# Output projection of a decoder block as seven products of quarters instead of one product

## The reference

```
(shift, scale, gate) = c @ W_mod + b_mod
u = x * (1 + scale) + shift
[q|k|v|z_a|B|C|xc|z_b|g_a|g_b] = u @ W_in
y_a = differential attention of q, k, v, 8 heads, RMS norm, * silu(z_a)
y_b = B * causal_conv3(C * xc) * silu(z_b)
h   = sigmoid(g_a) * (y_a @ P_a) + sigmoid(g_b) * (y_b @ P_b)
out = h @ W_out                                    # 512 x 2048 times 2048 x 2048
r   = 2**0.25 * x + gate * out
y   = (r - mean(r)) * rsqrt(var(r) + 1e-5) * ln_gain + ln_bias
```

## Time and profile before

| | us |
|---|---|
| median of 3 runs | 1496.1 (1493.0 to 1501.31) |
| the profiled execution, device time | 1492.94 |
| its span, first to last instruction | 1491.0 |
| matmuls in the output stage O0 | 768 |
| PE busy in the span | 1469.9 |

### The profile page before, as it was taken

One profiled execution on the slowest core, in us unless ns is written; L12 is line 12 of the kernel. 1 busy time (PEld: TensorE's weight loads), 2 busy tenths in 40 slices (PEclk: granted clock), 3 DMA queues, 4 the chain that ended last, 5 costly groups with the idle time before them and its releaser, 6 DMA issues.

```text
span 1491.0 us, 18556 instructions
## 1 busy us (share of the span) xinstructions
PE 1469.9 (99%) x6648; PEld 1212.9 (81%) x6648; DVE 887.9 (60%) x1234; ACT 525.0 (35%) x764; POOL 54.3 (4%) x101
## 2 busy tenths in 40 slices
PE   7999999999999999999999999999999999999996
PEld 6788888888888888888888888888887888788885
DVE  6988852286584865848658486585335233534447
ACT  2334532343543435434354343542231212421120
POOL 0000000000001000010000100000000000000000
PEclk9999999999999999999999999999999999999998
DMA  9999542352535525355253552524522322463222
GB/s 356 392 344 324 178 128 85 92 163 78 162 91 169 162 79 160 91 169 161 81 159 91 169 161 80 160 92 148 197 85 85 113 84 90 161 258 112 84 85 113
DMA packets 213164, 223.47 MB, mean 150 GB/s; under 512 B 8577, under 2 KB 160513, under 8 KB 212353
## 3 DMA queue, kind: packets, MB, share of 16 engines
q1 hardware_dynamic: 200736, 176.72, 36.1%
q0 software_dynamic: 11280, 39.85, 8.5%
q10 hardware_dynamic: 1106, 6.32, 1.0%
HBM read 213.43 MB, written 9.44 MB: 149 GB/s over the span
## 4 chain that ended last, share of the span: by engine, by line
PE 96%; DVE 2%; DMA 1%; issue 0%; ACT 0%; SPq 0%; DVEq 0%; ACTq 0%; POOLq 0%
PE acc L1468 30%; PE acc L1469 30%; PE acc L1470 30%; PE sc L1613 1%; PE sc L1468 1%; DMA raw<-in_w_in 1%; PE sc L1470 1%; PE sc L1469 1%; PE sc L1622 1%; PE misc L1470 1%; PE misc L1468 1%; PE misc L1469 1%; PE sc L1533 0%; DMA sig_b<-g_late 0%; DVE w_lo L908 0%
## 5 line engine op out<-in xcount | busy, mean ns | idle before, releaser
L1468 PE MATMUL acc<-act_hi,w_hi 128*128 128x512 f32 x1344 | 528.3, 393 | 2.2 <-DVE act_lo L983 2.2
L1470 PE MATMUL acc<-act_hi,w_lo 128*128 128x512 f32 x1344 | 524.1, 390 | 0.0
L1469 PE MATMUL acc<-act_lo,w_hi 128*128 128x512 f32 x1344 | 523.9, 390 | 0.0
L586 ACT ACTIVATE w_hi<-raw 128x1024 fp32r<-128x1024 f32 (+2 forms) x258 | 267.9, 1045 | 704.7 <-PE acc L1470 560.4
L908 DVE TENSOR_TENSOR w_lo<-raw,w_hi 128x1024 fp32r<-128x1024 f32 x254 | 306.3, 1214 | 330.5 <-ACT w_hi L586 328.6
L1468 PEld LDWEIGHTS acc<-act_hi,w_hi 128*128 128x128 f32 x1344 | 252.8, 188 | 57.7 <-DVE act_lo L983 3.0
L1470 PEld LDWEIGHTS acc<-act_hi,w_lo 128*128 128x128 f32 x1344 | 252.7, 188 | 53.3
L1469 PEld LDWEIGHTS acc<-act_lo,w_hi 128*128 128x128 f32 x1344 | 252.9, 188 | 51.8 <-issue 0.2
L1468 PE MATMUL acc<-w_hi,act_hi 128*128 128x512 f32 x368 | 143.3, 389 | 0.0
L1470 PE MATMUL acc<-w_hi,act_lo 128*128 128x512 f32 x368 | 143.2, 389 | 0.0
L1469 PE MATMUL acc<-w_lo,act_hi 128*128 128x512 f32 x368 | 143.2, 389 | 0.0
(11 more groups left out here) (212 smaller groups left out, 1150.0 us busy)
## 6 DMA issues: line engine op xcount, KB each, us to landing
raw<-in_w_in SPq DMA_DIRECT2D x258, 256.0 KB, 6.7
raw<-in_w_tail SPq DMA_DIRECT2D x32, 1024.0 KB
raw<-in_w_in SPq DMA_DIRECT2D x25, 1024.0 KB
w_mod_in<-in_w_mod SPq DMA_DIRECT2D x32, 512.0 KB, 8.8
w_mod_in<-in_w_mod SPq DMA_DIRECT2D x16, 1024.0 KB, 7.6
gate_in<-in_w_mod POOLq DMA_DIRECT2D x32, 512.0 KB, 4.1
bias_w<-in_w_in POOLq DMA_DIRECT2D x48, 256.0 KB, 3.3
res<-in_x ACTq DMA_DIRECT2D x1, 4096.0 KB, 13.6
```

Of the source, the lines that this page charges most:

```text
L586: return act.activation(dst, src, ACT.Copy)
L1468: pe.matmul(dst, a_hi, b_hi, start=first, stop=False)
L1469: pe.matmul(dst, a_hi, b_lo, start=False, stop=False)
L1470: return pe.matmul(dst, a_lo, b_hi, start=False, stop=last)
```

## The change

The output projection is cut into quarters: the 2048 rows of W_out into two halves (B1x, B2x), its columns into two (Bx1, Bx2), and `h` into two halves of tokens and two of rows (A11, A12, A21, A22), each quarter of `h` 256 tokens by 1024. Seven products replace eight. With S1 = A21+A22, S2 = S1-A11, S4 = A12-S2, S3 = A11-A21 and T1 = B12-B11, T2 = B22-T1, T3 = B22-B12, T4 = T2-B21 (signs are turned in places), their order is A11 B11, A12 B21, S1 T1, S2 T2, S4 B22, S3 T3, A22 T4; below they are called M0 to M6.

- A product has eight steps. A step is 128 rows by 1024 columns of weights (again 1024 elements for each partition) and 12 matmuls: four banks (2 token tiles by 2 column blocks) by 3. M6 goes bank by bank instead of step by step.
- Two sets of four banks are used: `acc`, and `sc` with `misc`. M3, M5 and M6 go on in the banks of M0, and M4 in those of M2. ACT copies a partial result out (`keep`, M0, M2 and M3), and DVE adds or subtracts a finished one (`join`, after M1, M4 and M5). M2 waits for the join after M1, and M6 for the join after M5.
- Plain quarters of weights (M0, M1, M4) come in pieces of 0.5 MB through a ring of four places in `raw`. B12 (4 MB) goes into `chain`. The sums are made there: ACT turns the sign, and POOL issues DMAs of 0.5 MB that add to what is in SBUF (`accum_op`), eight for M2, eight for M3, eight for M5 (into the ring) and eight for M6, at most four in flight. Six more add `x` to a gated quarter of `res`, two add `ln_bias`.
- The sums of `h` are made by DVE (`sums_of_h`).
- `gate` is divided by ALPHA, so that `x` is added as it is, and the norm's epsilon by ALPHA squared. For the first two token tiles ACT does the normalization (`Identity` with scale and bias, 2048 elements), DVE multiplies by `ln_g`, and a DMA adds `ln_bias`.
- `h_hi` and `h_lo` of whole tiles go; `hi_part` and `lo_part` (two each for a product, 1024 elements) come.

The ACT program (cut):

```diff
+            def turn_t2(i):
+                r = piece_of(S3_T3, i)
+                before = RING[(r - SLOTS) // HK]
+                act.wait_ge(lo_ready, step_of(before, (r - SLOTS) % HK) + 1 + RAW_START)
+                act.activation(ring(r), chain[:, i], ACT.Copy, scale=-1.0).then_inc(t3_begun, 1)
+                act.wait_ge(lo_ready, step_of(S2_T2, i) + 1 + RAW_START)
+                act.wait_ge(t3_begun, i + 1)
+                act.activation(chain[:, i], chain[:, i], ACT.Copy, scale=-1.0).then_inc(t2_turned, 1)
...
-                    round_at(S0, 0, 0, 4 * e + s + LEAD)
+                    if 4 * e + s + LEAD < 4 * SHORT:
+                        round_at(S0, 0, 0, 4 * e + s + LEAD)
+                    else:
+                        out_hi(A11_B11, 4 * e + s + LEAD - 4 * SHORT)
                     if s == 0:
                         act.wait_ge(late_back[e], 16)
                         for n in range(4):
                             act.activation(sig_b[:, n, :], sig_b[:, n, :], ACT.Sigmoid).then_inc(sig_ready, 1)
-                    if e == 0:
-                        act.wait_ge(half_done, S0 + BASE)
-                        h_hi(2 * s)
-                        h_hi(2 * s + 1)
-                    else:
-                        h_hi(8 + s)
+                    elif e == 0 and s < 3:
+                        hi_part(A11_B11, s - 1)
+                    if e == 1:
+                        turn_b12(s)
...
+            for i in range(5):
+                out_hi(S4_B22, i)
+            keep(S2_T2, "C12")
+            out_hi(S4_B22, 5)
+            hi_part(S3_T3, 0)
+            turn_t2(0)
+            out_hi(S4_B22, 6)
+            hi_part(S3_T3, 1)
+            turn_t2(1)
+            out_hi(S4_B22, 7)
+            turn_t2(2)
+            turn_t2(3)
+            for i in range(4):
+                out_hi(S3_T3, i)
+                turn_t2(4 + i)
```

The DVE program from M5 on:

```diff
+            for i in range(4):
+                out_lo(S3_T3, i)
+            join(S4_B22, "C12")
+            times_gate("C12", 1)
+            out_lo(S3_T3, 4)
+            lo_part(A22_T4, 0)
+            out_lo(S3_T3, 5)
+            lo_part(A22_T4, 1)
+            for i in (6, 7):
+                out_lo(S3_T3, i)
+            for i in range(4):
+                out_lo(A22_T4, i)
+            stats_of("C12")
+            settle()
+            for t in range(2):
+                spread(t)
+            for i in (4, 5, 6):
+                out_lo(A22_T4, i)
+            join(S3_T3, "C22")
+            out_lo(A22_T4, 7)
+            times_gate("C22", 2)
...
+            last_quarter(0)
+            for t in range(2):
+                dve.wait_ge(z_made, t + 1)
+                for c0 in (0, MID):
+                    dve.tensor_tensor(res[:, t, c0:c0 + MID], res[:, t, c0:c0 + MID], ln_g[:, c0:c0 + MID], ALU.mult
+                                      ).then_inc(scaled, 1)
+            stats_of("C22")
+            dve.wait_ge(ln_b_in, 16)
+            for t in (2, 3):
+                for j in ((1,) if t == 2 else (2, 3)):
+                    last_quarter(j)
+                settle()
+                spread(t)
```

POOL's queue, and PE's waits:

```diff
+            def add_weights(m, i, row, col):
+                e = added(m, i)
+                if e >= 4:
+                    pool.wait_ge(added_in[e % 4], 16 * (e // 4))
+                k = row * HK + i
+                dst = ring(piece_of(m, i)) if m == S3_T3 else chain[:, i]
+                pool.dma_start(dst, w_tail[k * P:(k + 1) * P, col * MID:(col + 1) * MID].rearrange(
+                    "p (a c) -> p a c", a=2), accum_op=ALU.add).then_inc(added_in[e % 4], 16)
...
+            for i in range(HK):
+                pool.wait_ge(t3_begun, i + 1)
+                add_weights(S3_T3, i, 0, 0)
+                pool.wait_ge(t2_turned, i + 1)
+                add_weights(A22_T4, i, 1, 0)
+            add_x("C12", 1)
+            add_x("C22", 2)
...
+            def wait_bank(m, j):
+                if m == A11_B11:
+                    pe.wait_ge(bank_drained[j], S_BLOCK0 + SHORT + BASE)
+                elif m == S1_T1:
+                    pe.wait_ge(m_added, j + 1)
+                elif m in (S2_T2, S4_B22, S3_T3):
+                    pe.wait_ge(m_copied, 4 * (m - S2_T2) + j + 1)
+                elif m == A22_T4:
+                    pe.wait_ge(m_added, 8 + j + 1)
```

More of the change, by code:

```diff
@@ new lines, in keep, with turn_b12 @@
+            def keep(m, name):
+                for j in range(4):
+                    if j < 3:
+                        act.wait_ge(m_full, 3 * m + j + 1)
+                    else:
+                        act.wait_ge(half_done, step_of(m + 1, 0) + BASE)
+                    copy(quarter_of(name, j // 2, j % 2), bank(m, j)).then_inc(m_copied, 1)
+            def turn_b12(n):
+                act.wait_ge(chain_in[n], 16)
+                both = chain[:, 2 * n:2 * n + 2, :, :]
+                act.activation(both, both, ACT.Copy, scale=-1.0).then_inc(b12_turned, 1)
@@ L868, in _ @@
[L868 to L879, removed]
@@ new lines, in _ @@
+            keep(S2_T2, "C12")
[11 more added lines that the diff above has]
+                turn_t2(4 + i)
+            out_hi(S3_T3, 4)
+            hi_part(A22_T4, 0)
+            out_hi(S3_T3, 5)
+            hi_part(A22_T4, 1)
@@ L886, in _ @@
+            for t in range(2, NT):
+                root(t)
         @block.vector
@@ L1365, in _, with out_lo @@
             close(4 + HEADS)
[L1368 to L1371, removed]
+            def out_lo(m, i):
+                f = step_of(m, i)
+                dve.wait_ge(hi_ready, f + 1)
+                end = m == A22_T4 and i < HK // 2
+                dve.tensor_tensor(w_end_lo[:, i] if end else w_lo[:, f % SLOTS], weights(m, i),
+                                  (w_end_hi[:, i] if end else w_hi[:, f % SLOTS]).bitcast(F32), ALU.subtract
+                                  ).then_inc(lo_ready, 1)
@@ new lines, in wait_full, with join @@
+            def wait_full(m, j):
+                if j < 3:
+                    dve.wait_ge(m_full, 3 * m + j + 1)
+                else:
+                    dve.wait_ge(half_done, step_of(m + 1, 0) + BASE)
+            def join(m, name):
+                for j in range(4):
+                    dst = quarter_of(name, j // 2, j % 2)
+                    wait_full(m, j)
+                    dve.wait_ge(m_copied, {"C11": 0, "C22": 4, "C12": 8}[name] + j + 1)
+                    if name == "C12":
+                        ins = dve.tensor_tensor(dst, dst, bank(m, j), ALU.subtract)
+                    else:
+                        ins = dve.tensor_tensor(dst, bank(m, j), dst, ALU.add if name == "C11" else ALU.subtract)
+                    ins.then_inc(m_added, 1)
@@ new lines, in _ @@
+            lo_part(S1_T1, 0)
+            out_lo(A12_B21, 5)
+            lo_part(S1_T1, 1)
+            out_lo(A12_B21, 6)
+            for b in range(2):
+                sums_of_h(S2_T2, b)
+            out_lo(A12_B21, 7)
+            for i in range(3):
+                out_lo(S1_T1, i)
+            join(A12_B21, "C11")
+            for i in (3, 4):
+                out_lo(S1_T1, i)
+            lo_part(S2_T2, 0)
+            out_lo(S1_T1, 5)
+            lo_part(S2_T2, 1)
+            out_lo(S1_T1, 6)
```

413 lines of the change are left out of this document (309 added, 104 removed).

## The result

| | before | after |
|---|---|---|
| time, median of 8 runs | 1493.49 us (1492.67 to 1501.31) | 1507.13 us (1505.40 to 1508.19) |
| ratio of times, 95% interval | | 1.0081 [1.0065, 1.0098] |
| span of the profiled execution | 1491.0 us | 1506.3 us |
| matmuls | 6648 | 6552 |

The kernel became 0.8% slower: 96 matmuls fewer, and 13.6 us more between the medians (12.1 us by the ratio). Forecast was 1494.5 us, no change. What came is the first rival, slower by the price of the adding transfers, which had a chance of 0.30 and 1504 to 1507 us. That 1507.13 lies at the edge of these bounds is partly luck: they were counted from a median before of 1496.1 us, where eight runs gave 1493.49, and as a change of span the rival said 8 to 11 us, where 15.3 came.

What follows compares the result with a forecast made beforehand. PE was taken as the bound: span 1491.0 - 21.8 (matmuls) + 0.6 (M0) + 0.6 (M2) + 7.9 (M5) + 6.5 (M6) + 2.8 (tail) + 1.5 (adds) = 1489.3; from the 1496.1 median, 1494.5 us, range 1484 to 1511.

Steps and rivals of the forecast that it cites:

- the first rival: Adding transfers on POOL's queue from M4's sixth step are the bound; at 2.47 us each 1504 to 1507 us; chance 0.30.
- M1 term: M1 waits some 1.5 us because eight adds, its plain pieces and `ln_g` share the DMA engines.
- The transfers that add: Step bounding a 0.5 MB add between 1.24 us (plain) and 2.47 us (twice the bytes); added 1.5 us at M1.
- I take 2.1: Price chosen for each 0.5 MB add, 2.1 us, because the second read doubles but the write doesn't.
- the prediction's own inequality: Between M4's sixth step and M6, 18 adds are in time only up to 2.1 us each.
- the third rival: Second `sig_b` comes 2 us later, M0 starts 2 to 3 us later, 1497 us; chance 0.45 together with the forecast.
- M5, ACT's order: In M5 hi, lo and two turns run in series, 4.42 us a step where PE needs 2.72: +7.9 us.
- M6, DVE's order: Before M6, DVE has 23.8 us without a gap from M5's lo 3 to the join: PE waits +6.5 us.
- The clock: PE's clock may fall after 6.5 us standing before M6; up to 2.8 us that costs nothing, DVE being behind.
- The tail: After M6, DVE's last quarter starts 2.8 us after PE's end, then 11.4 us as before: +2.8 us.
- The second rival: PE stays the bound, stalls of M5 and M6 half or less and DVE's tail lateness gone: 1484 us; chance 0.25.
- The sum with no price for adding: Span of 1487.7 us from matmuls saved and the waits at M0, M2, M5, M6 and tail, without M1's 1.5.

Runs made afterwards that it cites:

- plain_all: The changed kernel with every adding transfer made a plain one of the same bytes, sums left out: 1494.32 us, ratio 0.9990 to the kernel before.
- loads_later: The changed kernel with SP's loads of `ln_g` and of `x` for C21 moved behind four pieces of M4: 1503.43 us, ratio 1.0055 to the kernel before.
- entry: The changed kernel with ACT's turns of B12 behind the first three hi, DVE's first sum of `h` behind the draining: 1505.93 us, ratio 1.0066.
- orders: `loads_later` plus reordered ACT hi and turns, M5's and M6's adds, DVE joins and C12 statistics, M6's weights in order: 1497.15 us, ratio 1.0006.
- parked2: `entry` plus four -T2 pieces made in M3 in empty buffers, adds begun earlier, turns and adds reordered, 2 MB loads later: 1486.05 us, ratio 0.9940.

## Why the prediction was wrong, by its own steps

Where each product began, by the prediction's sum with its M1 term of 1.5 us, and in the trace:

| mark | predicted | measured | behind |
|---|---|---|---|
| M0 starts | 1305.9 | 1307.7 | 1.8 |
| M1 starts | 1329.2 | 1333.2 | 4.0 |
| M2 starts | 1351.6 | 1357.3 | 5.7 |
| M5 starts | 1417.0 | 1422.6 | 5.6 |
| M6 starts | 1453.0 | 1467.1 | 14.1 |
| PE ends | 1474.8 | 1491.9 | 17.1 |
| end | 1489.3 | 1506.3 | 17.0 |

**The step that failed is "The transfers that add", and in it "I take 2.1".** An add cost 2.49 us, the upper of the two bounds worked out from the rows (2.47). The reason given for 2.1, that only the read is doubled and the write isn't, did not make it cheaper: the engines were full at half the rate of plain pieces. By the prediction's own inequality, from 2.1 us on M5's last hi and C12's sums come late, and they did, M5's hi by far the more: the two later waits in M5 and the longer stand before M6 are what `plain_all` takes away. The middle value was moreover the one at which nothing is late, a choice that should have made me look twice; with the upper end the sum was 1499 to 1502 of span. A second term was too low, what the clock costs; it is priced below. The rule that stood beside it is told of the adding step of a ReduceScatter, which has two source reads on one ring and so half the rate of a copy, measured there at 1.93 times (the Trainium skill, "Collectives: The Full Stack", The bandwidth ceiling). The runs agree with its factor: 2.49 for 1.24 us is 2.0. That the two reads are the cause, no run here shows.

**M1's wait** was the same mis-sized price: 1.5 us taken, 3.5 measured (4.3 at 2.47 us by the prediction). Its sum was also taken at its low end: 8 x 2.1 and ten pieces at 1.24 to 1.45 us are 29.2 to 31.3 us in a stretch of 28, so 1.2 to 3.3. `loads_later` and `plain_all` each take the wait away. Between M1 and M2 the wait came as worked out, 0.4 us for 0.6, but M1's matmuls took 1.7 us more than 21.8, which the sum didn't have: the clock was down after the wait.

**M0** came 1.8 us late: `sig_b`'s second round starts on ACT at 1294.11, not 1292.2. Half of the 1.9 us is that POOL issued its load at 1287.16 and not 1286.2, since `h` was added up at 1286.8 and not 1285.8; the other half is that ACT had it 6.95 us after the issue, not 6.0, which is the third rival (2 to 3 us), right in kind. In `entry` `sig_b` comes as late (1294.17) and PE doesn't wait: the orders of ACT and DVE remove the wait. What that is worth, some 2 us by the ratios, is not clear of the noise.

**M5, ACT's order** was right: round 4.45 for 4.42 us, waits of PE 1.5, 1.6, 1.6 and 2.9 us for 1.35, 1.70, 1.70 and 3.1. What came on top is two waits for adds (3.4 us; all of these counted from start to start, less 0.23) and matmuls further apart (3.9 us).

**M6, DVE's order.** The prediction had DVE work 23.8 us without a gap from its fourth lo of M5 to the join. It took 31.8, with four gaps:

```profile
1434.50 1.22 DVE L1631 TENSOR_TENSOR w_lo<-raw,w_hi 128x1024 fp32r<-128x1024 f32 x1 [3.23 <-ACT w_hi L758]
...
1443.86 1.22 DVE L1631 TENSOR_TENSOR w_lo<-raw,w_hi 128x1024 fp32r<-128x1024 f32 x1 [1.20 <-ACT w_hi L758]
...
1448.79 1.23 DVE L1631 TENSOR_TENSOR w_lo<-raw,w_hi 128x1024 fp32r<-128x1024 f32 x1 [2.57 <-ACT w_hi L758]
1453.81 1.23 DVE L1631 TENSOR_TENSOR w_lo<-raw,w_hi 128x1024 fp32r<-128x1024 f32 x1 [3.79 <-ACT w_hi L758]
...
1460.13 2.47 DVE L1691 BATCH_NORM_STATS2 stats<-res 128x6 f32<-128x512 f32 x4 [0.56 <-DMA res<-in_x]
```

Three wait for hi that themselves wait for adds (7.6 us), the fourth is C12's statistics waiting for their `x` (0.6). These 8.1 us are the whole of the 8.0 that were not counted, and in `plain_all` they are gone. So of the 14.1 us by which M6 begins late, 8.0 are adds in M5, 2.1 the adds at M1, 1.8 M0's start and 1.7 the slower matmuls of M1; 0.5 is spread over small differences.

**The clock.** The prediction allowed that it falls after the stand before M6 and put it at nothing up to 2.8 us, with DVE behind PE. It cost 2.8 us and was not covered: DVE waited 3.49 us for the bank. It fell too after M1's wait of 3.5 us (0.72 as the mean of 1333 to 1339) and late in M5 (1.00 from 1425 to 1437, 0.84 from 1437 to 1448); after M0's wait of 3.0 us it stayed at 1.00, though in `plain_all` it fell there (0.77 from 1312.6 to 1320). M5 took 36.8 us from 1422.64 to its last matmul where 21.8 were counted; its six waits, counted in the same way, make 11.1 of the 15.0, the rest, 3.9, is matmuls further apart. These 3.9 us cost PE and not the kernel: M6 waited for DVE's join, which the adds had made late. The first rival's 1499 to 1502 of span had the adds nearly right (4.3 us at M1 for 3.5, 7 behind it for 8.0), left out M0's 1.8 and the clock's 1.7 and 2.8, and its upper end came out 4 us too low. No run changed the clock alone, so its share is read from the trace and not tested.

**The tail.** The stand before M6 was 7.4 us for 6.5. From PE's end to the end of the program it took 14.4 us, 14.5 by the sum, and from the last quarter on 11.3, 11.4 before.

**The second rival** (PE stays the bound) fell with `plain_all`: even with plain transfers 14.5 us of waits stay. The sum with no price for adding is 3.3 us less span than before; by its ratio `plain_all` is 1.5 us less [3.6 less to 0.6 more]. From M5's start to M6's it takes 35.8 us, 36.0 by the sum. From M0 to the end it takes 184.6, 181.8 by the sum, and the rest is slower matmuls after the waits before M0 and M6. So the orders were sized well, and the one resource that no row showed decided.

Open: what each of the changes in `orders` and in `parked2` is worth alone; and whether DVE's 5.5 us before M6 in `parked2` can be spread without POOL.

## What to carry to other kernels

In these runs a transfer that adds into SBUF took the DMA engines as long as two plain ones: count it as twice its bytes in the budget of each stretch, and where a row bounds it from both sides and one end changes the sign of the result, forecast from the end that a second source supports, not from the middle. Where such adds bunch up, their order doesn't shorten them; begin them a product earlier in buffers that are empty by then, and keep other large loads out of their stretch. A product saved is worth its matmuls only if its operands are ready at PE's pace, and a stand of PE can cost again through the clock (2.8 us after one of 7.4). Whether a slower PE costs the kernel anything is read from who releases the next stage: in M5 it cost nothing.

## What the runs showed of the hardware

- Adds of 0.5 MB from POOL's queue, four in flight: 2.49 us each, 205 to 218 GB/s with the engines full, landing after 9.4 us; plain ones in the same place land after 5.3 us.
- POOL spends 0.84 us on issuing an add of 0.5 MB, and 0.53 us on a plain transfer of that size (`plain_all`).
- A POOL product of 128x1024 takes 2.6 us. A DVE sum of 128x512 with both sources in SBUF beside it took 1.3 to 1.4 us, once 5.03, for 0.69.
- After a stand of over 7 us PE had 0.50 of its clock for 6 us; after one of 3.5 us the window from 1333 to 1339 us shows 0.72. After waits of 3.0 and 3.1 us before M0 it was 1.00 (1307.7 to 1313, kernel after) and 0.77 (1312.6 to 1320, `plain_all`).
